# Decoder block on Trainium2: ring slots, expert places, first expert transfers and the last group of experts rearranged

## The reference, cut to what matters

```python
x = x + merged @ w_out[l]
h2 = rmsnorm(x, ffn_norm[l])
x = x + moe(h2, ...)          # top 4 of 32 experts per token
return rmsnorm(x, final_norm)

# moe, for every expert e:
gu = hf @ w1[e] + b1[e]                       # w1[e]: 1024 x 2048
g_ = jnp.minimum(gu[:, :D_FF], 7.0)
u_ = jnp.clip(gu[:, D_FF:], -7.0, 7.0)
act = g_ * jax.nn.sigmoid(1.702 * g_) * (u_ + 1.0)
out = out + combine[:, e:e + 1] * (act @ w2[e] + b2[e])   # w2[e]: 1024 x 1024
```

## Time and profile before

| what | value |
|---|---|
| runs | 1115.7, 1116.76, 1117.56 us; median 1116.76 |
| profiled execution, own time | 1116.21 us |
| its span | 1114.4 us |
| mean granted TensorE clock | 0.988 |
| PE busy | 1021.7 us (92%) |
| PEld busy | 507.5 us (46%) |
| DVE, ACT busy | 301.1, 220.4 us |
| bytes moved | 437.23 MB, mean 392 GB/s |

### The profile page before, as it was taken

One profiled execution on the slowest core, in us unless ns is written; L12 is line 12 of the kernel. 1 busy time (PEld: TensorE's weight loads), 2 busy tenths in 40 slices (PEclk: granted clock), 3 DMA queues, 4 the chain that ended last, 5 costly groups with the idle time before them and its releaser, 6 DMA issues.

```text
span 1114.4 us, 12364 instructions
## 1 busy us (share of the span) xinstructions
PE 1021.7 (92%) x5014; PEld 507.5 (46%) x5014; DVE 301.1 (27%) x682; ACT 220.4 (20%) x377; POOL 18.2 (2%) x26
## 2 busy tenths in 40 slices
PE   5999999999999999898988888898989898989896
PEld 5987776434343434343434343434343343434343
DVE  4866576221212121212121211112121211111212
ACT  5555644111111111111111111011111110111112
POOL 1200020000000000000000000000000000000000
PEclk9999999999999999999999999999999999999998
DMA  9954379999999999999999999999999999999992
GB/s 346 349 190 151 114 285 392 427 427 426 428 426 418 426 437 431 430 428 431 433 433 432 431 431 432 432 429 433 431 432 429 433 433 433 433 429 432 431 432 103
DMA packets 31407, 437.23 MB, mean 392 GB/s; under 512 B 2905, under 2 KB 4113, under 8 KB 15761
## 3 DMA queue, kind: packets, MB, share of 16 engines
q1 hardware_dynamic: 29920, 431.53, 91.9%
q0 software_dynamic: 1168, 5.01, 1.1%
q10 hardware_dynamic: 288, 0.25, 0.1%
HBM read 435.73 MB, written 2.11 MB: 393 GB/s over the span
## 4 chain that ended last, share of the span: by engine, by line
PE 63%; DMA 32%; DVE 2%; issue 1%; ACT 1%; SPq 0%; DVEq 0%; ACTq 0%
DMA quad<-in_w 31%; PE bank L1291 26%; PE bank L1334 13%; PE bank L1016 6%; PE bank L1017 5%; PE bank L1018 5%; PE bank L1250 3%; PE bank L1207 1%; DMA ring<-in_w_in 1%; PE bank L1317 1%; PE bank L1300 0%; ACT r L616 0%; PE bank L1308 0%; PE bank L1006 0%; ACT r L637 0%
## 5 line engine op out<-in xcount | busy, mean ns | idle before, releaser
L1291 PE MATMUL bank<-quad,r 128*64 128x512 f32 x1536 | 348.3, 609 | 39.5 <-DMA quad<-in_w 39.5
L1291 PEld LDWEIGHTS bank<-quad,r 128*64 128x64 f32 x1536 | 116.0, 140 | 257.2 <-issue 240.8
L1334 PE MATMUL bank<-quad,r 128*64 128x512 f32 x768 | 170.1, 595 | 13.5 <-issue 8.8
L957 DVE TENSOR_SCALAR r<-bank 128x512 f32<-128x512 f32 x32 | 22.1, 692 | 415.5 <-PE bank L1291 415.5
L973 DVE TENSOR_TENSOR ysl<-bank,ysh 64x512 fp32r<-64x512 f32 x64 | 44.1, 688 | 300.8 <-ACT ysh L643 299.8
L630 ACT ACTIVATE r<-r 128x512 f32<-128x512 f32 x32 | 20.2, 631 | 480.2 <-DVE r L957 480.2
L1291 PE MATMUL bank<-place,r 128*64 128x512 f32 x512 | 111.8, 594 | 1.2 <-ACT r L616 1.2
L1334 PEld LDWEIGHTS bank<-quad,r 128*64 128x64 f32 x768 | 61.3, 137 | 108.6 <-issue 108.6
L643 ACT ACTIVATE ysh<-bank 64x512 fp32r<-64x512 f32 x64 | 37.9, 592 | 232.8 <-PE bank L1334 232.0
L680 DVE TENSOR_TENSOR wl<-ring,wh 128x1024 fp32r<-128x1024 f32 (+1 forms) x52 | 64.2, 1243 | 46.3 <-ACT wh L463 45.7
L1250 PEld LDWEIGHTS bank<-r,hs 128*128 128x128 f32 x544 | 63.3, 192 | 14.4 <-issue 13.7
(11 more groups left out here) (193 smaller groups left out, 783.5 us busy)
## 6 DMA issues: line engine op xcount, KB each, us to landing
quad<-in_w SPq DMA_DIRECT2D x72, 4096.0 KB, 29.9
place<-in_w SPq DMA_DIRECT2D x48, 2048.0 KB, 16.2
ring<-in_w_in SPq DMA_DIRECT2D x16, 1024.0 KB, 13.1
ring<-in_w_out SPq DMA_DIRECT2D x4, 1024.0 KB, 4.9
ring<-in_w_branch_pool SPq DMA_DIRECT2D x2, 1024.0 KB, 5.0
ring<-in_w_branch_attn SPq DMA_DIRECT2D x2, 1024.0 KB, 4.9
ring<-in_w_in SPq DMA_DIRECT2D x2, 768.0 KB, 10.4
xs<-in_x SPq DMA_DIRECT2D x2, 512.0 KB, 5.4
```

Source lines behind the costliest of these rows:

```text
L957: nc.vector.tensor_scalar(gclip, GA[:, :], LIMIT, None, ALU.min).then_inc(gclip_ready, 1)
L1291: ins = mm(bk[part, :], xgT[i // 2 % 2][:, k, own], w[:, c1:c1 + HALF], start=False, stop=k == KD - 1)
L1334: ins = mm(YT[part, :], a_k, w[:, kk, c1:c1 + HALF], start=k == 0, stop=k == KD - 1)
```

## The change

What it does:
- The ring has 3 slots in place of 7. The freed 4 MB are two places of 2 MB each, `o_early`, that no part of the front uses. Chunks 0 and 1 are issued into them among the ring loads, behind loads 11 and 13 (counted from 0).
- Chunk 2 goes into the place of chunk 0 before (`o_masks`), under the same condition, ahead of the last two ring loads. The other first uses get other homes and conditions: chunk 3 `merged`, chunk 4 low part 50, chunk 5 low part 52, chunk 6 `piece_used` 50, chunks 7 and 8 `piece_used` 52, chunk 9 the first gather. `xT` moves off `o_hT`, `wh` and `wl` lie in another order.
- Chunks 40 to 47 take the places 0, 1, 4, 5, 3, 6, 7, 8.
- The last group of experts is written out and loads 2 MB chunks. The last MB pairs of the last w1 and w2 chunk have a semaphore for each MB. The last expert's w2 comes by column halves (`w2_last`).
- The last expert has its own code: the first of its pair is scattered alone behind w1, no further gather, w2 by column halves, y copied as it is (not split), and one float32 matmul for each quarter with `gT2`, whose two halves of rows repeat the gates.
- The end is split between VectorE and ScalarE, with squares going to `junk` and the gain multiplied in before the root is known.
- The code of further rounds, which does not run with these inputs, is fitted to that.

```diff
-FRING = 7
+FRING = 3
@@
+        o_early = top[0]
+        top[0] += 2 * CHUNK
...
-        xT = at("xT", o_hT, KD * SEQ).rearrange("p (k t) -> p k t", k=KD)
+        xT = r1[:, 4352:6400].rearrange("p (k t) -> p k t", k=KD)
@@
-        first = [o_masks, o_bias + 3 * CHUNK, o_bias, o_gates, o_bias + CHUNK, o_bias + 2 * CHUNK,
-                 o_split, o_split + CHUNK, o_hT, o_xs]
+        first = [o_early, o_early + CHUNK, o_masks, o_gates, o_bias, o_bias + CHUNK, o_split, o_split + CHUNK, o_hT, o_xs]
...
-        order = [c % PLACES for c in range(4 * PLACES)] + [1, 5, 2, 4, 3, 6, 7, 8]
+        order = [c % PLACES for c in range(END - 2 * QUADS)] + [0, 1, 4, 5, 3, 6, 7, 8]
@@ sync
+                    if use in (12, 14):
+                        c = (use - 12) // 2
+                        chunk(0, c, place[c], chunk_loaded[c])
...
+                    if use == 24:
+                        sp.wait_ge(hmax_ready, 2 * NH)
+                        sp.wait_ge(piece_used, P_BA)
+                        chunk(0, 2, place[2], chunk_loaded[2])
                     load(use, wk[:, 2 * i:2 * i + 2, :], 2, D)
                     use += 1
...
             former_use = (
-                ((hmax_ready, 2 * NH), (piece_used, P_BA)),
-                ((low_ready, 42),),
-                ((logit_read, NH), (low_ready, 44)),
                 ((merged, 4),),
-                ((low_ready, 48),),
+                ((logit_read, NH), (low_ready, 50)),
                 ((low_ready, 52),),
+                ((piece_used, N_PIECES - 2),),
                 ((piece_used, N_PIECES),),
                 ((piece_used, N_PIECES),),
-                ((parts_done, 1),),
                 ((gather_done, 1),),
             )
...
-            with sp.Fori(FIRST, NE // GROUP) as g:
+            with sp.Fori(FIRST, GROUPS - 1) as g:
                 load_group(0, g)
+            for c in range(GROUP * CHUNKS):
+                e, j, i = NE - GROUP + c // CHUNKS, c % CHUNKS, halves[c % (2 * QUADS)][0]
+                former = 2 * (c - 2 * QUADS + 1) if c >= 2 * QUADS else 4 * (c // 2 - QUADS + 1)
+                sp.wait_ge(chunks_used, (NE - GROUP) * STEPS + former)
+                if e < NE - 1 or j < CHUNKS - 3:
+                    chunk(e, j, place[i], chunk_loaded[i])
+                elif j == CHUNKS - 2:
+                    sp.dma_start(place[i], w2_last[0, :, :]).then_inc(chunk_loaded[i], 16)
+                else:
+                    src, loaded = (w12[e, j // 2, :, CHUNK:], tail_loaded[0]) if j == CHUNKS - 3 else (w2_last[1, :, :], tail_loaded[1])
+                    sp.dma_start(place[i][:, 0:SLOT], src[:, 0:SLOT]).then_inc(chunk_loaded[i], 16)
+                    sp.dma_start(place[i][:, SLOT:CHUNK], src[:, SLOT:CHUNK]).then_inc(loaded, 16)
@@ scalar, end
-            squares(2, range(4))
+            squares(2, (0, 2, 1, 3))
+            for b in range(TB):
+                root(2, b)
+            for b, c, n in ((0, 1, 3), (1, 0, 2)):
+                half = slice(c * HALF, (c + 1) * HALF)
+                a.wait_ge(rstd_ready, 2 * 2 + b + 1)
+                a.wait_ge(scaled_ready, n)
+                nc.scalar.activation(hs[:, b, half], hs[:, b, half], ACT.Copy, scale=rstd[:, b:b + 1]).then_inc(out_ready, 1)
@@ vector
+                    if final and i == GROUP - 1:
+                        for c, bk in enumerate((UA, YT)):
+                            v.wait_ge(chunks_used, u * STEPS + KD + 2 * (c + 1))
+                            nc.vector.tensor_copy(yl[c], bk[:, :]).then_inc(y_low, 1)
+                        break
...
+            def scaled(n, q):
+                b, half = q // 2, slice(q % 2 * HALF, (q % 2 + 1) * HALF)
+                v.wait_ge(squares_ready, 4 * 2 + n + 1)
+                nc.vector.tensor_tensor(hs[:, b, half], YSUM[q][:, :], gfin[:, half], ALU.mult).then_inc(scaled_ready, 1)
+
+            scaled(0, 0)
+            scaled(1, 2)
+            square_sum(2, 0, 3)
+            scaled(2, 1)
             square_sum(2, 1, 4)
+            for b in range(TB):
+                inverse(2, b)
+            nc.vector.scalar_tensor_tensor(out=hs[:, 1, HALF:D], in0=YSUM[3][:, :], scalar=rstd[:, 1:2],
+                                           in1=gfin[:, HALF:D], op0=ALU.mult, op1=ALU.mult).then_inc(h_ready, 1)
+            v.wait_ge(scaled_ready, 1)
+            nc.vector.tensor_scalar(hs[:, 0, 0:HALF], hs[:, 0, 0:HALF], rstd[:, 0:1], None, ALU.mult).then_inc(h_ready, 1)
@@ tensor
+            def last_expert():
+                u = NE - 1
+                for k in range(KD):
+                    w = loaded_step(0, GROUPS - 1, GROUP - 1, k)
+                    if k == KD - 1:
+                        pe.wait_ge(tail_loaded[0], 16)
+                    for bk, c in ((GA, 0), (UA, F)):
+                        for part, c1 in ((lo, c), (hi, c + HALF)):
+                            ins = mm(bk[part, :], xgT[(GROUP - 1) // 2 % 2][:, k, hi], w[:, c1:c1 + HALF],
+                                     start=False, stop=k == KD - 1)
+                    ins.then_inc(chunks_used, 1)
+                scatter_even(u)
+                pe.wait_ge(act_ready, u + 1)
+                for c in range(4):
+                    ins = nc.tensor.transpose(GA[:, c * P:(c + 1) * P], act[:, c * P:(c + 1) * P], ident)
+                ins.then_inc(actT_done, 1)
+                pe.wait_ge(actT_ready, u + 1)
+                for c, bk in enumerate((UA, YT)):
+                    for k in range(0, KD, 2):
+                        if k % 4 == 0:
+                            w = loaded_step(0, GROUPS - 1, GROUP - 1, KD + 2 * c + k // 4).rearrange("p (k n) -> p k n", k=4)
+                        if c and k == KD // 2:
+                            pe.wait_ge(tail_loaded[1], 16)
+                        for part, kk in ((lo, k), (hi, k + 1)):
+                            a_k = actT[:, (kk % 4) * P + (kk // 4) * SLOTS:(kk % 4) * P + (kk // 4 + 1) * SLOTS]
+                            ins = mm(bk[part, :], a_k, w[:, kk % 4, :], start=k == 0, stop=k == KD - 2)
+                        if k % 4:
+                            ins.then_inc(chunks_used, 1)
+                pe.wait_ge(gT2_ready, 2)
+                for c in range(2):
+                    pe.wait_ge(y_low, 2 * u + c + 1)
+                    for b in range(TB):
+                        mm(YSUM[2 * b + c][:, :], gT2[:, b * P:(b + 1) * P], yl[c], start=False, stop=True,
+                           skip_group_check=True).then_inc(scattered, 1)
```

More of the change, by code:

```diff
@@ L200, in hybrid_block @@
         o_split = top[0]
-        wh = new("wh", LOOK * PIECE, f32r).rearrange("p (i n) -> p i n", i=LOOK)
-        wl = new("wl", LOOK * PIECE, f32r).rearrange("p (i n) -> p i n", i=LOOK)
+        wh, wl = [], []
+        for i in range(0, LOOK, 2):
+            for tiles, name in ((wh, "wh"), (wl, "wl")):
+                tiles += [new(f"{name}{i + j}", PIECE, f32r) for j in range(2)]
         o_hT = top[0]
@@ L283, in hybrid_block @@
             plan.append((i, len(uses) + 1, uses[-1] if uses else None))
[L284 to L287, removed]
+        halves = plan[END - 2 * QUADS:]
+        slots = [(first[halves[2 * n][0]] - o_bias) // (2 * CHUNK) for n in range(QUADS)]
+        assert sorted(slots) == list(range(QUADS))
+        for n, (i, _, _) in enumerate(halves):
+            assert first[i] == o_bias + (2 * slots[n // 2] + n % 2) * CHUNK
         gain_free = 2 * (1 + max(c for c, i in enumerate(order) if first[i] == o_masks))
@@ L647, in _ @@
+            copy_xgT(1, 0, 0)
+            a.wait_ge(combT_done, 1)
+            for half in (slice(0, NE), slice(NE, 2 * NE)):
+                nc.scalar.activation(combT[half, :], bank[3][0:NE, 0:SEQ], ACT.Copy).then_inc(combT_ready, 1)
+            copy_xgT(2, 1, 0)
+            with a.Fori(0, GROUPS - 1) as g:
+                expert_group(0, g)
+            expert_group(0, GROUPS - 1, final=True)
             a.wait_ge(count_ready, 1)
@@ L977, in _ @@
+            make_picks(0)
+            v.wait_ge(counts_done, 1)
+            link(nc.vector.tensor_reduce(cmax, bank[3][0:1, 0:NE], X, ALU.max))
+            assert routed[0] == R_COUNT
+            nc.vector.tensor_copy(count, cmax).then_inc(count_ready, 1)
+            with v.Fori(0, GROUPS - 1) as g:
+                expert_group(0, g)
+            expert_group(0, GROUPS - 1, final=True)
             v.wait_ge(count_ready, 1)
@@ L1301, in expert @@
                        start=False, stop=True, skip_group_check=True)
-                if late and i % 2 == 0 and not (written_out and e == 0):
+                if late and i % 2 == 0 and not (opening and i == 0):
                     scatter(u)
@@ L1309, in expert @@
                     ins.then_inc(gT_done, 1)
+                    if final and i == GROUP - 2:
+                        for b in range(TB):
+                            ins = nc.tensor.transpose(YT[lo, SEQ + b * P:SEQ + (b + 1) * P], gpick[:, b, hi], ident)
+                        ins.then_inc(gT2_done, 1)
```

(6 more changed lines are left out.)

243 lines of the change are left out of this document (130 added, 113 removed).

## The result

| | before | after |
|---|---|---|
| median of the runs | 1116.8 us (4 runs) | 1110.08 us (1108.83 to 1111.29, 4 runs) |
| profiled execution, own time | 1116.21 | 1108.83 |
| its span | 1114.4 | 1107.0 |
| last byte of weights landed, E | 1092.9 | 1091.9 |
| from E to the end of the span | 21.4 | 15.2 |

The ratio of after to before is 0.994, 95% interval 0.9924 to 0.9955: faster by 6.7 us, where 11.0 was forecast, and 0.8 us outside the stated range. The changed kernel was measured twice more, in later series on two chips: 0.9948 (0.9934 to 0.9961) and 0.9943 (0.9929 to 0.9957).

The account below looks back on a forecast made before the run. It took TensorE to bound the front and early expert pairs, and the transfer stream the late ones. Early chunks -3.2 and the tail -7.8 made -11.0 us, from 1116.8 to 1105.8 us, range 1103.5 to 1109.3.

Parts of the forecast that it names:

- What bounds the kernel: Whole kernel: front and early expert pairs bound by TensorE (53.3 us a pair), late pairs by the stream (58.3 us).
- rival 2: Early transfers: the whole of the moved bytes is gained, 9.8 us, giving 1099.2 us; chance 0.06.
- The ring of 3 slots: Front: the smaller ring costs 0, with load 12 landing 3.7 us before it is needed.
- The stream at chunk 14: End of the front: chunk 14 lands 3.2 us earlier, 225.0 for 228.2, and this is kept to the end.
- chunk 13 lands at 219.8: Before chunk 14: the stream gets there in time, since chunk 14's own bytes can begin only at 220.1.
- The term for b1 and b2: Stream from chunk 3 to chunk 13: some 1.5 us for the 0.6 MB that go beside it.
- The last group: Last experts: more instructions and 2 MB issues in place of 4 MB cost nothing while 8 places are outstanding.
- The tail: From the last byte's landing (E', after the change) to the end: 13.7 us for 21.5, a gain of 7.8.
- rival 3: End: low clock (+1.8 us) or VectorE's skip at its upper bound (+1.6), 1107.4 to 1109.3 us; chance 0.2.
- The clock: End: TensorE runs at full clock; a low stretch like the one before would cost 1.7 to 1.9 us.
- The signs of being wrong: Last byte moved by under 2 or over 4 us, front ending late, or over 15 us behind the last byte.
- The first: Rival: a gate or late chunk between 161 and 220 us leaves only the tail's gain, 1109.0 us; chance 0.13.

Follow-up runs that it names:

- after_again: The changed kernel run again with nothing edited: 1110.27 us, ratio 0.9948 to the kernel before.
- half_b1: The changed kernel with the load of b1 (512 KB) and the first MB of chunk 4 both issued earlier: 1109.74 us, ratio 0.9943.
- no_rounds: The changed kernel without the code of the further rounds, and so without every engine's skip over it: 1110.08 us, ratio 0.9948.
- tail_only: The kernel before with only the new last group and end, keeping its ring of 7 slots and first transfers: 1111.46 us, ratio 0.9960.

## Why the prediction missed

- **What bounds the kernel** held: front by TensorE, early pairs by TensorE, late pairs by the stream; and that the moved bytes would not come out in full (rival 2) held.
- **The ring of 3 slots** held: no wait of a split for a ring transfer after the first, TensorE busy 84.18 of 85 us in the same window. Load 12, behind chunk 0, landed at 72.3, 3.3 us before ScalarE took it up at 75.6 (3.7 predicted).
- **The stream at chunk 14** was mis-sized: -3.2 predicted, -1.5 measured in the changed kernel, lined up by the chunk's own issue. The step that failed is "chunk 13 lands at 219.8 ... with 0.3 us to spare": it landed at 221.5 in after_again. From the issue of chunk 3 that is 60.2 us for 58.2. The term for b1 and b2, 1.5, is the largest error: the start of the run took 3.0 more than even. The spacing of 4.905 for 4.88 adds 0.25, late landings at chunks 8 and 13 add 0.9, and the gap of 0.6 before chunk 9 did not show. The kernel before had the same 3.0 (chunk 3 lands 8.9 us after its issue, chunk 4 6.2 later), so its trace could have told. Nor was chunk 14 the narrowest gate: had the bytes come in time, chunk 9 and what follows it would have held chunk 14 at 9.1 us after its issue (half_b1). The spare of 0.3 us was too little to rest 3.2 us on.
- **The last group** is the step that failed outright: "more instructions in the written-out group, and 2 MB issues in place of 4 MB ... both cost nothing". The stream came out 1.8 to 2.4 us longer: 1.1 is from the size (24 chunks at 4.905 for 12 quads at 9.72), shown in every profile, and 0.7 to 1.3 from one late landing beside a code fetch, whose cause is argued. The question asked was whether the queue runs dry. In a stretch bound by bytes on end the question is what each byte costs.
- **The tail** was -7.8 predicted, -6.3 to -7.1 measured. Step by step from E' in after_again: VectorE at -7.7 (predicted -7.9), w2 at -3.5 (-3.6), last matmul ends +7.3 (+7.1), last sum +8.2 (+8.3), last output issued +11.5 (+10.95), end +14.8 (+13.7). All of the miss is in the outputs, and no_rounds, free of the fetch there, ends at +13.6. In the prediction the skip's cost was looked for on VectorE (rival 3), where it was hidden, and not at the transfers. The Trainium skill (Runtime: NRT & Kernel Launch, Instruction fetch mechanics) speaks of a stall of the engine that branches; here TensorE was done with its last matmul at 1100.1 when it fetched at 1102.7 (after_again), and the outputs of another queue were late.
- **The clock** stayed at its upper level through the tail, as taken (granted clock 1.00 from 1077 to 1101 us in all three profiles).
- **The signs of being wrong** that the prediction named did show: E moved by about 1 us in the first profile and not by 2 to 4, and the tail was 15.2, over 15.
- **Rivals.** The first (tail only, 1109.0) came nearest in mechanism at the last byte: the stream ended where it had been, though by two errors that cancel, about 1.5 us gained in front and given back in the last group. That they cancel is chance. The third's upper end (1109.3) is nearest in number, and its kind of thing did happen, a slow end by some 1 us, but in the outputs and not in the clock or in VectorE's skip.

Sum of the measured terms for after_again against before: -1.8 at chunk 14 (0.3 of it since the chunk was issued that much earlier), +1.8 in the stream, -6.7 in the tail, -6.7 in the span; the medians say -6.7, -6.4 and -6.6.

## What to carry to other kernels

Where transfers run on end, count everything that goes through the transfer engines, and the size of each transfer; measure the spacing of landings in the trace of before rather than adding it up from bytes. Where a shift rests on a gate, follow the whole run of gates before it and distrust a margin of tenths. A half of a change that gives the expected number has still to be read in its trace: tail_only met its 2.2 us half by accident. A finer last transfer is worth its cost only where the engine behind it would otherwise wait for the whole: it must reach back far enough (here to the expert before the last) that the engine is not already behind when the last piece lands. And compare the moment at which TensorE's clock opens before putting a shift of the whole timeline down to a change.

## What the runs showed that I had not expected

- The opening of TensorE's clock in the front moves the whole timeline: 1.6 us between two executions of the changed kernel (matmuls at the pace of 2.4 GHz from 15.5 us in one, from 18.8 in the other).
- 2 MB transfers (16 KB a row) stream at 4.905 us each, 4 MB ones (32 KB a row) at 9.72, so 1% faster for the same bytes: 427 against 432 GB/s in the window of the last group.
- With code fetched beside the outputs the tail is 0.7 to 1.9 us longer than without (14.3 to 15.5 us against 13.6), either by a long issue or by a late landing.
- From the landing of chunk 14 to that of the sixth quad the stream took 222.9 to 223.0 us before, after and with each half alone, however the late landings were spread on the way: a late landing in one place was made up in another.
